# Three blocks on one core: latent keys before first scores, split pieces between heads, turned probabilities copied before rows, square sums after a split

## Chip, cores and metric

The kernel runs on one core of a Trainium2 chip. The metric is the device time of one launch in microseconds (us). TensorE does the matrix products, VectorE (DVE) and ScalarE (ACT) the work on their results, GpSimd (POOL) small steps, SyncE (SP) starts the loads of the weights. The five run their own lists of instructions in order and wait for each other on semaphores.

## What is computed

Three residual blocks over 256 tokens of width 1024, in fp32. The first has MoBA attention and retention, cross attention to a memory, and a gated MLP. The second has a sparse attention with an index, a short convolution and a squared-ReLU MLP. The third has latent attention (MLA) and a squared-ReLU MLP. The part on which most of the change lies is MLA, cut from the reference:

```python
def _mla_mixer(h, rope_mla, w_dq, q_norm, w_uq, w_dkv, kv_norm, w_ukv, w_o):
    q = (_rms_norm(h @ w_dq, q_norm) @ w_uq).reshape(bsz, s, C_HEADS, C_NOPE_DIM + C_ROPE_DIM)
    q_rope = _rotate(q[..., C_NOPE_DIM:], cos, sin)
    kv_a = h @ w_dkv
    c_kv = _rms_norm(kv_a[..., :C_KV_RANK], kv_norm)
    k_rope = _rotate(kv_a[..., C_KV_RANK:][:, :, None, :], cos, sin)[:, :, 0, :]
    kv = (c_kv @ w_ukv).reshape(bsz, s, C_HEADS, C_NOPE_DIM + C_V_DIM)
    k_nope, v = kv[..., :C_NOPE_DIM], kv[..., C_NOPE_DIM:]
    ...
```

There are 16 heads; a head's query and key have 64 elements of their own and 32 rotated ones, and the 32 of the key are the same for all heads. Every sublayer ends in `x = x + rms_norm(...)`.

## The kernel before

**Precision.** A product in fp32 is made of three products in a faster format. Each weight is split into a high part `w_hi` (ScalarE, L630) and a low part `w_lo` (VectorE, L1181, L1184 or L1187 by the kind of weight), and the rows likewise (L648, L1202); TensorE adds hi·hi, lo·hi and hi·lo (`products`, L1786).

**Weights.** They come in units of up to 1 MB through a ring of four: SP loads a unit when VectorE has split the one four places earlier (`w_low`), and ScalarE splits a unit when TensorE has used the one four places earlier (`w_used`). `split_to(u)` in the lists of ScalarE and VectorE marks where unit u is split; its place among the other work is written by hand, and so is all other order. `e` is the first unit of MLA's query weights. Units e to e+5 are the queries' (`uq`), e+6 and e+7 the keys' and values' (`ukv`, four pieces of 512 columns on each engine), e+8 to e+11 the output projection (`odd_out`, two pieces of 1024 columns).

**Attention.** `attention(a, heads)` stands in the lists of three engines and is a pipeline over heads. In step n TensorE makes the scores of head n (L1893), turns the probabilities of head n-2 (L1901) and multiplies those of head n-3 with the values (L1910). VectorE masks the scores and takes their maximum (`masked_max`, L1339; in cross attention L1343 and L1345) and copies the turned probabilities of head n-2 to SBUF (`copy_turned`, L1351); ScalarE makes the exponentials (L801). In the steps H and H+1 behind the last head VectorE also makes the first half of the output rows, of tokens 0 to 127 and then 128 to 255 (`normalise_half`, L1368 and L1369), and TensorE turns them for the output projection (`turn_half`, L1855). `copied()` is TensorE's wait until ScalarE has moved the projection's sums out of PSUM (`evict`, L688).

**MLA's start.** `keys(g)` (L2382) and `values_of(g)` (L2391) make the keys and values of the heads 8g to 8g+7; `copy_keys` and `copy_values` (L1124 and L1129 on ScalarE, L1711 and L1716 on VectorE) bring them to SBUF. `rotate_queries(g, t)` (L1248 to L1253) rotates the queries of half g and tokens t, `turn_heads(g)` (L1855) turns them, and `plain_banks` (L672, L1220) copies these. `spread_rope` on GpSimd (L557) copies the rotated part of the key from head 0 to the other 15 heads.

**Squared MLP.** `first_up` makes the hidden rows of chunk 0 by tokens, ScalarE takes them out (`first_part`, L860), VectorE squares them (L1436); then `second_up` (L2064, L2068) makes chunk 1 from the units u0+2 and u0+3. `boundary` adds the sublayer's output to x, and its two `stream_square` (L710) sum x's squares, for a factor that the MLP needs at its end.

## Time and profile before

| what | value |
|---|---|
| median of 3 runs | 1043.85 us (1043.06 to 1043.96) |
| the profiled execution | 1043.6 us, span of its trace 1041.8 us |
| TensorE busy | 1018.8 us, 98% of the span |
| VectorE, ScalarE, GpSimd busy | 673.0, 568.5 and 87.2 us |
| granted TensorE clock | 0.998 of full speed (2.4 GHz) |
| DMA | 176.32 MB, 169 GB/s on average |

An engine's busy time is the sum of its instructions' spans. The chain that ended last is made of TensorE for 95% of the span, so a microsecond is gained only where TensorE stands idle, or lost where a new wait appears. A row of the view of waits tells for a group of instructions what ended the idle time just before them. In the timeline a row gives start, length, engine, line, operation and the tiles; the bracket at its end is the engine's idle time before it and what ended that.

### The profile page before, as it was taken

The page shows a single profiled execution, that of the slowest core. Times are in us where ns is not written, and L with a number is a line of the kernel's source. Part 1 is how long each engine was busy: PE and PEld are TensorE (multiplying, and loading weights), DVE is VectorE, ACT ScalarE, POOL GpSimd, SP SyncE. Part 2 cuts the span into 40 slices and gives each one's busy share as a digit, 9 for nine tenths or more (in the row PEclk, how much of TensorE's full clock was granted, in tenths as well). Part 3 has the DMA queues.
Part 4 walks back from the last instruction along what each step waited for, and adds up shares of the span by engine and source line. Part 5 has one row for each costly group of instructions (what it writes and reads, how often), then busy time and mean ns, then how long its engine had stood idle before and what let it go on. Part 6 is the DMA issues. An engine that isn't in the chain of part 4 may idle for free.

```text
span 1041.8 us, 14292 instructions
## 1 busy us (share of the span) xinstructions
PE 1018.8 (98%) x5164; PEld 862.5 (83%) x5164; DVE 673.0 (65%) x1083; ACT 568.5 (55%) x909; POOL 87.2 (8%) x117
## 2 busy tenths in 40 slices
PE   7999999999999999999999999999998999999997
PEld 6888888888888888788888888888898888888886
DVE  5575675457556554869856676566579767756663
ACT  7466465427545444766555665455476566554541
POOL 2010001001000000300051200000052001000000
PEclk9999999999999999999999999999999999999999
DMA  9746236315545555463423555554255044654521
GB/s 351 289 162 242 79 114 224 130 41 182 189 175 212 175 205 173 157 239 125 164 117 127 217 202 191 195 182 169 84 189 216 1 162 163 242 196 176 192 81 41
DMA packets 28463, 176.32 MB, mean 169 GB/s; under 512 B 3248, under 2 KB 3392, under 8 KB 9984
## 3 DMA queue, kind: packets, MB, share of 16 engines
q1 hardware_dynamic: 26784, 170.08, 45.1%
q0 software_dynamic: 1456, 5.48, 1.4%
q8 instruction: 30, 0.49, 0.2%
q10 hardware_dynamic: 176, 0.13, 0.0%
q14 instruction: 17, 0.14, 0.0%
HBM read 174.62 MB, written 1.05 MB: 169 GB/s over the span
## 4 chain that ended last, share of the span: by engine, by line
PE 95%; DVE 2%; ACT 1%; issue 1%; DMA 1%; SPq 0%; DVEq 0%; ACTq 0%
PE PS L1786 67%; PE PS L2064 10%; PE PS L2068 5%; PE PS L1855 3%; PE PS L1893 3%; PE PS L1910 3%; PE PS L2298 1%; PE PS L1901 1%; DMA x<-in_x 1%; DVE w_lo L1184 1%; PE PS L2000 0%; ACT w_hi L630 0%; PE PS L2382 0%; PE PS L2391 0%; PE PS L1941 0%
## 5 line engine op out<-in xcount | busy, mean ns | idle before, releaser
L1786 PE MATMUL PS<-w_hi,hT 128*128 128x512 f32 (+2 forms) x1296 | 323.2, 389 | 2.2 <-issue 1.6
L1187 DVE SCALAR_TENSOR_TENSOR w_lo<-w_raw,gcol,w_hi 128x512 fp32r<-128x512 f32 (+4 forms) x318 | 260.9, 879 | 92.3 <-ACT w_hi L630 90.6
L630 ACT ACTIVATE w_hi<-w_raw,gcol 128x512 fp32r<-128x512 f32 (+4 forms) x326 | 244.4, 817 | 96.4 <-PE PS L1786 69.6
L1786 PEld LDWEIGHTS PS<-w_hi,hT 128*128 128x128 f32 x1296 | 237.8, 188 | 47.4 <-issue 1.7
L1181 DVE TENSOR_TENSOR w_lo<-w_raw,w_hi 128x1024 fp32r<-128x1024 f32 x118 | 143.3, 1249 | 91.4 <-ACT w_hi L630 90.4
L630 ACT ACTIVATE w_hi<-w_raw 128x1024 fp32r<-128x1024 f32 x118 | 119.2, 1052 | 102.7 <-PE PS L1786 97.5
L1786 PE MATMUL PS<-w_lo,hT 128*128 128x512 f32 (+2 forms) x648 | 171.8, 384 | 0.0
L2064 PE MATMUL PS<-hT,w_hi 128*128 128x512 f32 x448 | 156.6, 398 | 1.4 <-ACT arena L860 1.4
L1786 PEld LDWEIGHTS PS<-w_lo,hT 128*128 128x128 f32 x648 | 120.8, 188 | 23.6
L2068 PE MATMUL PS<-hT,w_lo 128*128 128x256 f32 x448 | 116.6, 281 | 0.0
L1786 PE MATMUL PS<-w_hi,gT_hi 128*128 128x512 f32 x408 | 114.0, 392 | 0.0
L1786 PE MATMUL PS<-w_lo,gT_hi 128*128 128x512 f32 x408 | 112.7, 389 | 0.0
L1786 PE MATMUL PS<-w_hi,gT_lo 128*128 128x512 f32 x408 | 112.7, 389 | 0.0
L2064 PEld LDWEIGHTS PS<-hT,w_hi 128*128 128x128 f32 x448 | 81.5, 188 | 18.2 <-issue 2.2
L1786 PEld LDWEIGHTS PS<-w_hi,gT_lo 128*128 128x128 f32 x408 | 76.6, 188 | 16.1
L1786 PEld LDWEIGHTS PS<-w_lo,gT_hi 128*128 128x128 f32 x408 | 76.5, 188 | 15.9
L1786 PEld LDWEIGHTS PS<-w_hi,gT_hi 128*128 128x128 f32 x408 | 76.4, 188 | 15.2
L2068 PEld LDWEIGHTS PS<-hT,w_lo 128*128 128x128 f32 x448 | 84.7, 189 | 4.5
L517 POOL TENSOR_SCALAR msq<-ssq 128x1 f32<-128x1 f32 (+1 forms) x31 | 10.5, 338 | 809.6 <-ACT work L710 746.8
L1202 DVE TENSOR_TENSOR hT<-PS,hT 128x512 fp32r<-128x512 f32 (+2 forms) x46 | 29.4, 668 | 29.6 <-ACT hT L648 29.4
L648 ACT ACTIVATE hT<-PS 128x512 fp32r<-128x512 f32 (+2 forms) x46 | 25.4, 582 | 40.7 <-PE PS L1855 40.6
L801 ACT ACTIVATE work<-work,attention_bias 128x128 f32<-128x128 f32 x64 | 28.5, 447 | 27.2 <-DVE attention_bias L1339 27.2
(191 smaller groups left out, 842.8 us busy)
## 6 DMA issues: line engine op xcount, KB each, us to landing
w_raw<-in_w SPq DMA_DIRECT2D x64, 1024.0 KB, 4.8
w_raw<-in_w_gu SPq DMA_DIRECT2D x22, 1024.0 KB, 4.8
w_raw<-in_w_in SPq DMA_DIRECT2D x11, 1024.0 KB, 7.5
w_raw<-in_w_dn SPq DMA_DIRECT2D x22, 512.0 KB, 4.5
w_raw<-in_w_mem_k SPq DMA_DIRECT2D x4, 1024.0 KB, 4.8
w_raw<-in_w_out SPq DMA_DIRECT2D x4, 1024.0 KB, 4.9
w_raw<-in_w_cq SPq DMA_DIRECT2D x4, 1024.0 KB, 4.7
w_raw<-in_w_mem_v SPq DMA_DIRECT2D x4, 1024.0 KB, 4.8
```

What stands on the lines that cost most here:

```text
L630: act.activation(high, source, ACT.Copy, scale=1.0 if col is None else gcol[:, col + TURNED * k:col + TURNED * k + 1])\
L648: act.activation(d, PS[:, 4 + n["tb"] % 4, 0:blocks * P].rearrange("p (b m) -> p b m", m=P), ACT.Copy).then_inc(tb_high, 1)
L801: ins = act.activation(a.E[hd % 3][:, c0:c1], src, ACT.Exp, bias=a.nb[:, hd, t:t + 1], scale=-1.0 if a.masked else a.scale, accum_out=a.su ...
L1181: ins = dve.tensor_tensor(lo, raw, hi, ALU.subtract)
L1187: ins = dve.scalar_tensor_tensor(out=lo, in0=raw, scalar=gcol[:, col + TURNED * k:col + TURNED * k + 1], in1=hi, op0=ALU.mult, op1=ALU.sub ...
L1202: dve.tensor_tensor(lo, PS[:, 4 + n["tb"] % 4, 0:blocks * P].rearrange("p (b m) -> p b m", m=P), hi.bitcast(F32), ALU.subtract).then_inc(t ...
L1786: mm = pe.matmul(bank(t, j)[:, 0:width], rows[:, kc0 + k, tok], w[:, s, at:at + width], start=begin and i == 0, stop=end and i == 2)
L1855: mm = pe.transpose(PS[0:rows, 4 + n["tb"] % 4, i * P:(i + 1) * P], src, ident[:])
L1893: mm = pe.matmul(PS[:, a.score_bank + hd % 2, c0:c1], q, k, start=i == 0, stop=i == len(pairs) - 1)
L1910: mm = pe.matmul(out_banks(a, t)[:, hd * a.dv:(hd + 1) * a.dv], a.ET[hd % 2][:, c0 + s * P:c0 + (s + 1) * P], a.v(hd, s), start=s == 0, st ...
L2064: return pe.matmul(PS[:, 4 + b, :], w_hi[:, s, at:at + P], hT[:, k, :, :].rearrange("p s m -> p (s m)"), start=k == 0, stop=k == KC - 1)
L2068: return pe.matmul(PS[:, 4 + b, 0:SEQ], w_lo[:, s, at:at + P], hT_hi[:, k, :], start=False, stop=False)
```

## The change

It has five parts. (1) In MLA, TensorE makes `values_of(0)` before `turn_heads(1)` and `keys(1)` before the first scores; the waits for copied keys and values are placed later or split by engine, and the rotated key is spread by one DMA that ScalarE starts, in place of five copies on GpSimd. (2) The units e+9, e+10 and e+11 are split in halves, one half ahead of every second head (`split_half`); before, e+9 was split at the start of the heads, and e+10 and e+11 behind them. (3) `copy_turned` stands ahead of `normalise_half`. (4) The wait `copied()` moves in MoBA, cross attention and the sparse attention (`dsa`) to a place inside step 3, ahead of the first values. (5) In the squared MLPs unit u0+3 is split ahead of `first_part(0)`, the sums of x's squares come after that, and `second_up` waits for each of its units only where it uses it.

```diff
@@ gpsimd
-            def spread_rope():
-
-                tb_done(pool, KEY_BANK)
-                for head in range(1, 16, 3):
-                    pool.tensor_copy(kT4[64:96, head:head + 3, :], kT4[64:96, 0:1, :].to_broadcast([32, 3, SEQ])).then_inc(rope_spread, 1)
...
@@ scalar
+            def split_half(u, half):
+
+                assert n["split"] == u and len(pieces(u)) == 2
+                split(u, some=slice(half, half + 1))
+                n["split"] += half
...
-                stream_square(0)
-                stream_square(1)
+                if squares:
+                    stream_square(0)
+                    stream_square(1)
...
+                split_to(m.u0 + 3)
                 first_part(0)
-                split_to(m.u0 + 3)
+                for t in range(TT):
+                    stream_square(t)
                 first_part(1)
...
             high_keys(1)
             split_to(e + 6)
+            act.wait_ge(rope_copied, 1)
+            act.dma_start(kT4[64:96, 1:16, :], kT4[64:96, 0:1, :].to_broadcast([32, 15, SEQ])).then_inc(rope_spread, 16)
             n["used"] += 3
             evict(0, queries(1), query_rows)
...
             copy_keys(0)
             split_to(e + 8)
+            copy_values(0)
             plain_banks(4, heads96(qT4, 1))
-            copy_values(0)
-            split_to(e + 9)
-            attention(mla, [0])
             copy_keys(1)
-            attention(mla, [1])
+            attention(mla, [0, 1])
             copy_values(1)
-            attention(mla, range(2, mla.H), False)
+            attention(mla, [2, 3], False)
+            for k in range(6):
+                split_half(e + 9 + k // 2, k % 2)
+                attention(mla, [4 + 2 * k, 5 + 2 * k], False)
             high_halves(hT_hi)
-            boundary(4)
+            boundary(4, squares=False)
@@ vector
                     if hd < a.H:
                         masked_max(hd)
-                    elif rows is not None:
-                        normalise_half(a, rows, hd - a.H, 0)
                     if hd >= 2:
                         copy_turned(hd - 2)
+                    if hd >= a.H and rows is not None:
+                        normalise_half(a, rows, hd - a.H, 0)
...
+                split_to(m.u0 + 3)
                 first_part(0)
-                split_to(m.u0 + 3)
                 first_part(1)
...
             rotate_queries(1, 0)
+            split_to(e + 7)
             rotate_queries(1, 1)
-            split_to(e + 7)
             n["used"] += 8
             copy_keys(0)
+            copy_values(0)
             plain_banks(4, heads96(qT4, 1))
             split_to(e + 8)
-            copy_values(0)
-            attention(mla, [0])
-            split_to(e + 9)
             copy_keys(1)
-            attention(mla, [1])
+            attention(mla, [0, 1, 2])
             copy_values(1)
-            attention(mla, range(2, mla.H + 2), False, h)
+            attention(mla, [3, 4], False)
+            for k in range(6):
+                split_half(e + 9 + k // 2, k % 2)
+                attention(mla, [5 + 2 * k, 6 + 2 * k], False, h)
+            attention(mla, [mla.H + 1], False, h)
@@ tensor
                         turn_probs(hd - 2)
+                    if hd == 3 and free:
+                        free()
                     if hd >= 3:
                         values(hd - 3)
...
-                    for j in range(2):
-                        high_ready(u + j)
-                        split_ready(u + j)
                     for i, b in enumerate([1, 2, 0, 3]):
                         if i == 1:
                             turn_hidden()
                         pe.wait_ge(m.part if i < 2 else m.low, i % 2 + 1)
                         for j in range(2):
+                            if i == 0:
+                                high_ready(u + j)
+                                split_ready(u + j)
                             mm = up_block(u + j, j, b)
...
-            copied()
-            attention(dsa, [3])
+            attention(dsa, [3], free=copied)
...
             keys(0)
+            copied()
+            values_of(0)
             wait_h(2)
             turn_heads(1)
-            copied()
-            values_of(0)
             pe.wait_ge(keys_copied, 2)
-            pe.wait_ge(rope_spread, 5)
+            keys(1)
+            pe.wait_ge(rope_spread, 16)
             turned(8)
             attention(mla, [0])
-            keys(1)
             attention(mla, [1])
-            pe.wait_ge(values_copied, 2)
+            for t in range(TT):
+                pe.wait_ge(values_copied[t], 1)
             values_of(1)
             attention(mla, [2])
+            pe.wait_ge(values_copied[0], 2)
+            attention(mla, range(3, 8))
             pe.wait_ge(keys_copied, 4)
-            pe.wait_ge(values_copied, 4)
-            attention(mla, range(3, mla.H + 3), h)
+            attention(mla, range(8, 11))
+            pe.wait_ge(values_copied[1], 2)
+            attention(mla, range(11, mla.H + 3), h)
```

MoBA and cross attention get `free=copied` in the same way as `dsa`. VectorE's `split_half` does the low part of the same half as ScalarE's.

The order on TensorE at MLA's start, before (L2382 makes keys, L1855 turns queries, L2391 makes values, L1893 is the first head's scores):

```order
1228 L2382 MATMUL PS<-hT,w_lo 128x256 [waits w_low]
1229 L2382 MATMUL PS<-hT,w_lo 128x256
1230 L1855 MATMUL PS<-ident,h 96x128 [waits tb_free1,h_ready]
...
1237 L1855 MATMUL PS<-ident,h 96x128 x3
1238 L2391 MATMUL PS<-w_hi,hT 128x512 [waits acc_copied]
...
1242 L2391 MATMUL PS<-w_lo,hT 128x512 x2
1243 L1893 MATMUL PS<-arena 128x128 [waits tb_free0,tb_free1,tb_free3,tb_free2,rope_spread,keys_copied]
1244 L1893 MATMUL PS<-arena 128x256
1245 L2382 MATMUL PS<-hT,w_hi 128x256 [waits w_high]
```

The same place in the changed kernel (the lines are now L2401, L2410 and L1873):

```order
1228 L2401 MATMUL PS<-hT,w_lo 128x256 [waits w_low]
1229 L2401 MATMUL PS<-hT,w_lo 128x256
1230 L2410 MATMUL PS<-w_hi,hT 128x512 [waits acc_copied]
...
1234 L2410 MATMUL PS<-w_lo,hT 128x512 x2
1235 L1873 MATMUL PS<-ident,h 96x128 [waits tb_free1,h_ready]
...
1242 L1873 MATMUL PS<-ident,h 96x128 x3
1243 L2401 MATMUL PS<-hT,w_hi 128x256 [waits w_high,keys_copied]
```

The values of the first half stand ahead of the turns of the rotated queries, and the second half's keys behind these and ahead of all scores.

VectorE in MLA's heads 3 to 5, before (L1339 is `masked_max`, L1351 `copy_turned`):

```order
455 L1351 COPY work<-PS 128x384
456 L1339 ISA work,attention_bias<-PS,causal 128x128
457 L1339 ISA attention_bias 128x1
458 L1339 ISA work,attention_bias<-PS,causal 128x256
459 L1339 ISA attention_bias 128x1
460 L1351 COPY work<-PS 128x384
461 L1339 ISA work,attention_bias<-PS,causal 128x128
```

The same in the changed kernel (L1355, L1367), with a piece of the output projection's weights (L1190):

```order
456 L1367 COPY work<-PS 128x384
457 L1190 TENSOR_TENSOR w_lo<-w_raw,w_hi 128x1024
458 L1355 ISA work,attention_bias<-PS,causal 128x128
459 L1355 ISA attention_bias 128x1
460 L1355 ISA work,attention_bias<-PS,causal 128x256
461 L1355 ISA attention_bias 128x1
462 L1367 COPY work<-PS 128x384
```

Such a piece now stands behind every second head's copy, six in all.

VectorE at the end of cross attention, before (L1351 is `copy_turned`, L1368 and L1369 `normalise_half`, L1181 a split):

```order
118 L1351 COPY work<-PS 128x512
119 L1368 RECIPROCAL attention_sum<-attention_sum 128x4
120 L1369 TENSOR_TENSOR h<-PS,attention_sum 128x512
121 L1351 COPY work<-PS 128x512
122 L1369 TENSOR_TENSOR h<-PS,attention_sum 128x512
123 L1351 COPY work<-PS 128x512
124 L1181 TENSOR_TENSOR w_lo<-w_raw,w_hi 128x1024 x2
```

The same in the changed kernel:

```order
118 L1367 COPY work<-PS 128x512 x2
119 L1384 RECIPROCAL attention_sum<-attention_sum 128x4
120 L1385 TENSOR_TENSOR h<-PS,attention_sum 128x512
121 L1367 COPY work<-PS 128x512
122 L1385 TENSOR_TENSOR h<-PS,attention_sum 128x512
123 L1190 TENSOR_TENSOR w_lo<-w_raw,w_hi 128x1024 x2
```

Each of the two last copies stands ahead of the rows it followed.

## Rows read from the trace of the kernel before

**Rows 1.** Waits of TensorE: us in total, times, longest us
```profile
PE PS L1855 <- DVE h L1253: 1.4, 1, 1.4
PE PS L2064 <- ACT arena L860: 1.4, 2, 0.7
PE PS L1893 <- ACT arena L688: 1.2, 1, 1.2
PE PS L1910 <- DVE work L1351: 1.2, 1, 1.2
...
PE PS L1893 <- DVE arena L1220: 0.6, 1, 0.6
PE PS L1893 <- ACT h L688: 0.2, 1, 0.2
```

**Rows 2.** Timeline of cross attention's end: start, length, work, idle before
```profile
206.98 0.60 PE L1901 MATMUL PS<-ident,work 128*128 128x128 f32 x4
...
209.56 0.69 DVE L1369 TENSOR_TENSOR h<-PS,attention_sum 128x512 f32<-128x512 f32 x1
210.16 0.68 DVE L1351 COPY work<-PS 128x512 f32<-128x512 f32 x1
...
214.22 1.28 DVE L1202 TENSOR_TENSOR hT<-PS,hT 128x512 fp32r<-128x512 f32 x2
...
215.15 1.28 PE L1786 MATMUL PS<-w_hi,hT 128*128 128x512 f32 x4
```

**Rows 3.** Timeline of the sparse attention's step 3
```profile
536.33 1.11 ACT L688 ACTIVATE arena<-PS,rstd 128x1024 f32<-128x1024 f32 x1 [0.86 <-PE PS L1786]
...
538.59 0.78 PE L1910 MATMUL PS<-arena,work 128*128 128x64 f32 x6
```

**Rows 4.** Timeline of the first squared MLP's start
```profile
581.42 0.58 ACT L860 ACTIVATE arena<-PS 128x512 f32<-128x512 f32 x1
...
583.12 2.73 DVE L1187 SCALAR_TENSOR_TENSOR w_lo<-w_raw,gcol,w_hi 128x512 fp32r<-128x512 f32 x4
...
586.11 0.47 PE L2064 MATMUL PS<-hT,w_hi 128*128 128x512 f32 x1 [0.68 <-ACT arena L860]
```

**Rows 5.** One line's instructions, all of MLA's key and value splits: ns min/median/max
```profile
L1184 DVE SCALAR_TENSOR_TENSOR w_lo<-w_raw,gcol,w_hi x8: 744/747/1312, 782.3 to 792.8; 128x512 fp32r<-128x512 f32 x8
```

**Rows 6.** Timeline of MLA's start and of its output projection's
```profile
782.57 5.72 POOL L557 COPY arena<-arena 32x768 f32<-32x768 f32 x5 [5.47 <-DVE hT L1202]
...
792.66 1.17 PE L2391 MATMUL PS<-w_hi,hT 128*128 128x512 f32 x4
...
804.53 0.60 ACT L1129 ACTIVATE arena<-PS 128x512 f32<-128x512 f32 x1
...
805.23 0.89 PE L1893 MATMUL PS<-arena 128*128 128x128 f32 x4 [0.76 <-issue]
...
831.33 1.17 PE L1786 MATMUL PS<-w_hi,hT 128*128 128x512 f32 x4 [0.41 <-issue]
```

**Rows 7.** Timeline of one head of MLA
```profile
808.38 0.55 DVE L1351 COPY work<-PS 128x384 f32<-128x384 f32 x1
...
809.47 0.29 DVE L1339 CUSTOM_DVE_ANT_0 work<-PS,causal 128x128 f32<-128x128 f32 x1 [0.54 <-PE PS L1893]
809.60 0.78 PE L1910 MATMUL PS<-arena,work 128*128 128x64 f32 x6
...
809.87 0.40 ACT L801 ACTIVATE work<-work,attention_bias 128x128 f32<-128x128 f32 x1 [0.67 <-DVE attention_bias L1339]
...
811.25 0.78 PE L1910 MATMUL PS<-arena,work 128*128 128x64 f32 x6
```

**Rows 8.** Page, costliest groups: count, busy us, mean ns, idle before
```profile
L1181 DVE TENSOR_TENSOR w_lo<-w_raw,w_hi 128x1024 fp32r<-128x1024 f32 x118 | 143.3, 1249 | 91.4 <-ACT w_hi L630 90.4
L630 ACT ACTIVATE w_hi<-w_raw 128x1024 fp32r<-128x1024 f32 x118 | 119.2, 1052 | 102.7 <-PE PS L1786 97.5
```

**Rows 9.** Page, DMA issues: count, KB each, us from issue to landing
```profile
arena<-in_decay POOLq DMA_DIRECT2D x1, 512.0 KB, 10.8
```

More of the change, by code:

```diff
@@ L1167, in _, with split @@
             n = {"split": 0, "tb": 0, "high": 0, "copied": 0, "used": 0}
-            def split(u, it=None):
+            def split(u, it=None, some=range(KC)):
                 if u >= COUNT:
@@ L1174, in split @@
                 done = 0
-                for cols in pieces(u):
+                for part, cols in enumerate(pieces(u)):
+                    if part not in some:
+                        done += 1
+                        continue
                     lo, raw, hi = w_lo[:, u % RING, cols], w_raw[:, u % RAW, cols], w_hi[:, u % RING, cols].bitcast(F32)
@@ L1194, in split_to, with split_half @@
                     n["split"] += 1
+            def split_half(u, half):
+                assert n["split"] == u and len(pieces(u)) == 2
+                split(u, some=[half])
+                n["split"] += half
             def low_banks(count, dst):
@@ L2224, in _ @@
             attention(moba, [2])
-            copied()
-            attention(moba, range(3, moba.H + 3))
+            attention(moba, range(3, moba.H + 3), free=copied)
             retention(lambda: turn_half(mix, 0))
@@ L2252, in _ @@
             attention(cross, [2])
-            copied()
-            attention(cross, range(3, cross.H + 3), h)
+            attention(cross, range(3, cross.H + 3), h, copied)
             out_project(h)
```

27 lines of the change are left out of this document (13 added, 14 removed).

## Prediction

> **What bounds the kernel now.** I read the chain that ended last first: it is TensorE for nearly all of the span, so an edit on another engine counts only by a wait of TensorE that it removes or makes. The second view is therefore TensorE's own waits [rows 1]. Behind the start-up of the kernel they are short and few: 1.4 us for a rotation on VectorE (L1253, MLA), 1.4 us in two pieces for ScalarE's L860 (one in each squared MLP), 1.2 us for ScalarE's L688 (sparse attention), 1.2 us for VectorE's copy L1351 (cross attention), 0.6 us for the copy of turned queries L1220 (MLA), 0.2 us for L688 (MoBA). Two more are put down to "issue" and stand in the timeline of MLA: 0.76 us before the scores of head 3 and 0.41 us before the output projection [rows 6]. Together 7.2 us, 0.7% of the time. That is the ceiling, since the change leaves TensorE's products as they are and removes none. The third view is the timeline at each of these places, for what really ended the wait and what is late next.
>
> **Cross attention: copies ahead of rows.** The probabilities of head 2 are turned at 206.98, 0.60 us long, but VectorE waits for values before it makes rows at 209.56, and copies head 2 only at 210.16 [rows 2]. TensorE waits 1.2 us for that copy [rows 1]. With the copy ahead of the rows it runs at about 207.6 and the whole wait goes; TensorE would stand 1.3 us earlier behind head 3 (210.90, where its values began, less 209.6, where its turns end), and reach the output projection at 215.15 - 1.3 = 213.8. Late next is VectorE: its queue from the rows on is shorter by one copy, 0.6 us, so L1202, which makes the low part of the first rows, moves from 214.22 to 213.6, and its first half (0.64 us) ends at 214.3. The projection starts at 214.4 and not at 213.8: **0.75 us** of gain, not 1.3. Bounds: 0.6 (VectorE's shift alone) and 1.3.
>
> **Sparse attention: the wait `copied()` inside step 3.** The eviction L688 runs from 536.33 for 1.11 us, TensorE waits for it with the scores of head 3 and multiplies the first values at 538.59 [rows 3]. Only those values write what is being evicted. With the wait ahead of them the scores and turns, 1.1 us up to 538.59, fill the wait; their inputs, exponentials of heads 1 and 2 and VectorE's maxima, are older than the eviction. The values start at 537.5: **1.1 us**, bounds 0.8 and 1.2. What stands behind on ScalarE (the exponentials of head 3) has the gate's eight transposes as cover. In MoBA the same edit meets 0.2 us [rows 1], but there the exponentials of head 1 stand behind the eviction on ScalarE, and TensorE's next step needs them; I take nothing, at most 0.2 us. In cross attention the eviction is over when it is waited for: nothing.
>
> **Squared MLPs: split ahead, sums behind.** TensorE's wait of 0.68 us before `second_up` is put down to the second L860. It asks only for the first, whose row is at 581.42; what ended last for it is the split of u0+3 on VectorE, 583.12 and 2.73 us long, up to 585.85 [rows 4]. That split was late because ScalarE summed x's squares before it made the high part. Now the high part comes 2.5 us earlier, VectorE's low part follows the one before it without a break and ends at about 585.3, and TensorE asks for it only half a block (1.4 us) after its start. Both cover the 0.68 us. The sums are now between two steps on ScalarE, where about 3 us were split and idle time; VectorE's first square slips by nearly 3 us to 586.0, but is needed at 588.3, after TensorE's first block. Twice 0.68: **1.35 us**, bounds 0.7 and 1.4. Nothing on TensorE asks for the sums before the MLP's end.
>
> **MLA's start.** The waits of 1.4, 0.6 and 0.76 us go if nothing new is late: 2.8 us. The first one: values, twelve products of which four take 1.17 us [rows 6], some 3.0 us in all, now stand ahead of the turns that need the rotation. The rotation in its turn comes later, since a unit of four pieces stands before its second half: 4 x 0.68 = 2.7 us. It also comes earlier: the pieces of a unit took 744 to 1312 ns [rows 5], and the slow four lay beside GpSimd's copies from 782.57 on, 5.72 us long [rows 6]; without those copies I take 1.7 us off. The wait would be 1.4 + 2.7 - 1.7 - 3.0, below zero by 0.6. The Trainium skill ("SBUF — State Buffer", "Who interferes with whom") says that a VectorE instruction with two SBUF inputs contends with a GpSimd instruction that reads SBUF; by that rule, the trace agrees, and by its reverse (the pieces stay slow) the wait would be 1.1 us and the MLA term smaller by as much. The second wait, 0.6 us, now has the whole group of the second keys before it and goes. The third: scores of head 3 began when ScalarE's copy of values, 804.53 and 0.60 long, was done [rows 6]. It still waits for that copy, but this one now stands behind the exponentials of head 1, which start some 2.5 us earlier; I get 802.5 for its end and 802.4 for the scores. So the start gives **2.7 us**.
>
> **MLA's heads: pieces between.** A head takes 1.65 us (809.60 to 811.25), in which VectorE idles 0.54 and ScalarE 0.67 us [rows 7]. For two heads VectorE has 1.08 us free and gets a piece of 1249 ns, ScalarE 1.34 and gets 1052 [rows 8]; queued operations overlap by about 0.1 us, so both just fit. But the two are linked in a ring: VectorE's piece (1.14) delays the next maximum, the exponential starts 0.40 later (809.47 to 809.87), two heads' halves take 0.9, then ScalarE's next piece (1.08) before VectorE's next: 3.5 us, against 3.3 us for two heads. The slack of a copy, from 808.93 to its use at 809.60, absorbs the first piece or two; then about 0.15 us is lost for each of four pieces: 0.6 us. At the end the delay of 0.8 us meets the values of head 13, which no longer have a group of scores ahead of them as cover: 0.9 us. Copies ahead of rows return 0.4 us there, and the first half of the second bank's rows comes 0.2 us late in the projection. Sum of MLA: 2.7 - 0.6 - 0.9 + 0.4 - 0.2 = **1.4 us**. Bounds: 2.8 (pieces cost nothing) and -0.5 (a piece costs each of six pairs 0.2 us more than taken and the rotation is late by 0.8). Units e+10 and e+11 leave the place behind the heads, where TensorE did not wait for them: nothing. The DMA that replaces GpSimd's copies costs ScalarE its issue and the wait for one VectorE copy, some 0.5 us ahead of an eviction that nobody needs for 2 us.
>
> **Sum.** 0.75 + 1.1 + 1.35 + 1.4 = 4.6 us. The profiled execution took 1043.6 us, so 1039.0; the median of before is 0.25 us above that execution: **1039.3 us**.
>
> **Rivals.** (a) The pieces are free: the ring has more slack than I give it. For it: each engine alone has room. Against it: the ring's sum of 3.5 us. Then MLA gives 2.8 and the time is 1037.9. (b) The pieces fill VectorE: beside ScalarE's pieces and TensorE's traffic they take 1.3 us and more, as the slow ones in rows 5 did beside another engine, and the rotation is late too. MLA gives about -0.5, the time is 1041.2. (c) The gains are given back: an earlier TensorE meets other waits, for instance for splits or loads behind the boundaries. For it: several places where splits end shortly before their use. Against it: from the boundaries to the loops no wait of more than 0.7 us is shown, and loads have slack. About 1042.7. (d) Slower: the DMA of the rotated key is late. TensorE cannot begin any score without it. It is issued at about 782.1 (GpSimd's copies, which wait for the same row, began at 782.57 [rows 6]), when SP's queue loads weights, and moves 480 KB in rows of 1 KB; the first scores are reached at about 797 (802.4 less the second values and three heads' scores), 15 us later. The slowest comparable row, 512 KB in 10.8 us [rows 9], fits. From 797 every us late is a us lost, after 19.7 us the whole gain of 4.6 is gone, at 24 us of landing the time is 1048. The Trainium skill ("DMA: Bandwidth & Descriptors", "Rules for kernel authors") states that two transfers issued from two engines share the same DMA engines with their packets interleaved; by it the DMA takes turns with the 1 MB loads, which bears on (d), and no run here shows it yet. (e) The edits don't reach the chip as described: the order of instructions shows all of them, so I give it nothing.
>
> **Chances.** Forecast 0.60, (a) 0.13, (b) 0.14, (c) 0.08, (d) 0.05. The forecast's own bounds are 1038.3 to 1040.6. The range takes in most of (a) and (b): 1037.5 to 1041.6. A difference under 0.2% (2.1 us) can't be told from no change here. Faster than 1041.8 are the forecast, (a) and most of (b): 0.83; within are (c) and the rest of (b): 0.12; slower is (d): 0.05.
>
> **What would show it.** In TensorE's waits, the rows for L1253, L1220, L860 and L688 of the sparse attention are gone. In cross attention the projection starts 0.75 us earlier against the head's copy, after a wait for L1202 of about 0.5 us. In MLA, head 3's scores start 2.7 us sooner after the first keys than before, then pairs of heads take 3.3 to 3.5 us with waits of 0.15 us for L1351 in every second head, and one of near 0.9 us at head 13's values. The pieces of L1184 are all near 745 ns. Wrong would be: slow pieces with no GpSimd beside them, pairs at 3.7 us or more, or a wait for the DMA before the first scores.

## The result, and the profile after

The changed kernel took 1037.28 us (median of 4 runs, 1036.58 to 1038.33) beside 1043.87 us for the kernel before on the same chip: ratio 0.9937, 95% interval 0.9925 to 0.9949. A second set, beside the experiments, gave 1038.43 us (5 runs, 1037.40 to 1039.03) beside 1044.05: ratio 0.9943, 0.9929 to 0.9956. So the change gains 5.6 to 6.6 us. The forecast was 4.6 us and 1039.3 us, its range began at 1037.5: the direction was right, the size too small. The profiled execution took 1036.75 us, its trace spans 1034.9 us, with a granted clock of 0.999.

**Waits.** What ended TensorE's idle time in the changed kernel, behind its first load (columns: engine, tile and line, releaser, us in total, times, longest). Lines of the changed kernel: L1804 is the products' old L1786, L1913 the scores, L1921 the turns, L1930 the values, L1367 the copy of turned probabilities, L1385 the rows, L1873 the turns of rows.

```profile
PE PS L1804 <- issue: 1.5, 3, 0.6
PE PS L1804 <- DVE arena L1711: 0.7, 1, 0.7
PE PS L1930 <- DVE work L1367: 0.6, 1, 0.6
PE PS L1873 <- DMA x<-in_x: 0.5, 1, 0.5
PE PS L1930 <- ACT arena L688: 0.2, 1, 0.2
PE PS L1873 <- DVE h L1385: 0.2, 1, 0.2
```

Against [rows 1], the waits for the rotation (L1253), for L1220, the two for L860 and the one for L688 in MoBA are gone; of the one for L688 in the sparse attention 0.2 us is left and has moved to the values. The 0.6 us for L1367 is another wait than in rows 1: it stands at the values of MLA's head 13 and no longer in cross attention. Of the first row, 0.34 us is new and stands in cross attention; the other 1.15 us of it, in two waits, and the 0.7 us for L1711 stand in the kernel before as well. The change does not reach them, and the 7.2 us of the prediction leave them out.

**Where the time went.** TensorE's work is the same in both kernels but for its order at three places, so equal groups of products can be laid side by side: start before less start after. That difference grows where the change gains. It steps by 0.26 us at MoBA's step 3, by 0.80 in cross attention, 1.0 in the sparse attention and 0.93 in the first squared MLP. In MLA it rises by 3.4 us up to the scores of head 3, falls by 0.9 over the heads and by 0.7 at head 13's values, and rises by 0.4 in the output projection; the second squared MLP adds 0.9. Before all of these there is a step of 0.8 us within the first 16 us of the kernel, where the change edits nothing.

**The start-up.** TensorE's timeline there, the kernel before first (start us, length us, engine, line, operation, tiles, count), then two executions of the changed kernel, the one of the prediction's result and a second one:

```profile
11.38 2.06 PE L1786 MATMUL PS<-w_hi,hT 128*128 128x512 f32 x4
...
14.77 0.62 PE L1786 MATMUL PS<-w_lo,hT 128*128 128x512 f32 x2
```

```profile
11.22 1.53 PE L1804 MATMUL PS<-w_hi,hT 128*128 128x512 f32 x4
...
13.95 0.62 PE L1804 MATMUL PS<-w_lo,hT 128*128 128x512 f32 x2
```

```profile
11.34 2.06 PE L1804 MATMUL PS<-w_hi,hT 128*128 128x512 f32 x4
...
15.57 0.62 PE L1804 MATMUL PS<-w_lo,hT 128*128 128x512 f32 x2
```

The last row of each is the same pair of products. In the first execution of the changed kernel it begins at 13.95 us, in the second at 15.57, and behind it the two are shifted by 1.62 us and nothing else up to the end. The spans are 1034.9 and 1036.6 us. So the part of a span from this pair to the end is the measure that tells kernels apart: 1027.0 us before (1041.8 - 14.77), 1021.0 after (1034.9 - 13.95, and 1036.6 - 15.57). The change is worth **6.0 us**, and 0.8 us of the difference between the two first traces is chance of the start-up. I call this part "the rest".

### The profile page after: what moved, and what is told of

It reads as the page before. It is cut to its first block, busy times and chain, and to the rows that moved or that the text cites. A ratio compares the mean times of both kernels' runs of the same rounds, so it can differ in the third digit from the quotient of the medians.

```text
span 1034.9 us, 14294 instructions
## 1 busy us (share of the span) xinstructions
PE 1018.0 (98%) x5164; PEld 862.4 (83%) x5164; DVE 670.3 (65%) x1083; ACT 568.0 (55%) x909; POOL 82.4 (8%) x112
## 4 chain that ended last, share of the span: by engine, by line
PE 94%; ACT 2%; DVE 1%; issue 1%; DMA 1%; SPq 0%; DVEq 0%; ACTq 0%
PE PS L1804 68%; PE PS L2086 10%; PE PS L2090 5%; PE PS L1873 4%; PE PS L1913 2%; PE PS L1930 2%; PE PS L2318 1%; ACT w_hi L624 1%; PE PS L1921 1%; DMA x<-in_x 1%; ACT work L802 1%; PE PS L2401 1%; PE PS L2410 1%; PE PS L2022 0%; PE PS L1963 0%
## 5 line engine op out<-in xcount | busy, mean ns | idle before, releaser
L1804 PE MATMUL PS<-w_hi,hT 128*128 128x512 f32 (+2 forms) x1296 | 322.6, 389 | 2.2 <-issue 1.5
L1804 PEld LDWEIGHTS PS<-w_hi,hT 128*128 128x128 f32 x1296 | 237.5, 188 | 47.6 <-issue 1.5
L1190 DVE TENSOR_TENSOR w_lo<-w_raw,w_hi 128x1024 fp32r<-128x1024 f32 x118 | 143.7, 1250 | 92.4 <-ACT w_hi L624 91.5
L1804 PE MATMUL PS<-w_lo,hT 128*128 128x512 f32 (+2 forms) x648 | 171.6, 384 | 0.0
L1804 PEld LDWEIGHTS PS<-w_lo,hT 128*128 128x128 f32 x648 | 120.5, 188 | 23.5
L1804 PE MATMUL PS<-w_hi,gT_hi 128*128 128x512 f32 x408 | 114.0, 392 | 0.0
L1804 PE MATMUL PS<-w_lo,gT_hi 128*128 128x512 f32 x408 | 112.8, 389 | 0.0
L1804 PE MATMUL PS<-w_hi,gT_lo 128*128 128x512 f32 x408 | 112.7, 389 | 0.0
L1804 PEld LDWEIGHTS PS<-w_hi,gT_lo 128*128 128x128 f32 x408 | 76.6, 188 | 16.1
L1804 PEld LDWEIGHTS PS<-w_lo,gT_hi 128*128 128x128 f32 x408 | 76.5, 188 | 15.9
L1804 PEld LDWEIGHTS PS<-w_hi,gT_hi 128*128 128x128 f32 x408 | 76.4, 188 | 15.3
L518 POOL TENSOR_SCALAR msq<-ssq 128x1 f32<-128x1 f32 (+1 forms) x31 | 12.6, 405 | 815.0 <-ACT work L710 752.4
```

Of the source, the lines that this page charges most:

```text
L1190: ins = dve.tensor_tensor(lo, raw, hi, ALU.subtract)
L1804: mm = pe.matmul(bank(t, j)[:, 0:width], rows[:, kc0 + k, tok], w[:, s, at:at + width], start=begin and i == 0, stop=end and i == 2)
```

## Experiments

The edits are to the changed kernel. "Gives" is the rest of the trace, less 1021.0.

| run | median us | ratio to before, 95% interval | pair at us | rest us | gives us |
|---|---|---|---|---|---|
| before (profile) | 1043.87 | 1 | 14.77 | 1027.0 | +6.0 |
| the changed kernel | 1037.28 | 0.9937 (0.9925 to 0.9949) | 13.95 | 1021.0 | 0 |
| after_again | 1038.43 | 0.9943 (0.9929 to 0.9956) | 15.57 | 1021.0 | 0.0 |
| u_mlp | 1039.63 | 0.9961 (0.9947 to 0.9975) | 14.10 | 1022.9 | +1.9 |
| u_free | 1039.20 | 0.9956 (0.9940 to 0.9973) | 14.77 | 1022.3 | +1.3 |
| u_copy | 1039.14 | 0.9949 (0.9933 to 0.9966) | 15.47 | 1022.1 | +1.1 |
| u_mla | 1040.61 | 0.9966 (0.9954 to 0.9979) | 15.26 | 1023.4 | +2.4 |
| pool_spread | 1039.33 | 0.9955 (0.9939 to 0.9970) | 14.84 | 1022.8 | +1.8 |
| ring_cut | 1037.13 | 0.9933 (0.9918 to 0.9948) | 15.37 | 1020.0 | -1.0 |
| behind | 1040.09 | 0.9960 (0.9946 to 0.9975) | 14.83 | 1024.2 | +3.2 |
| two | 1037.16 | 0.9934 (0.9918 to 0.9949) | 14.70 | 1020.2 | -0.8 |
| two_cut | 1037.58 | 0.9932 (0.9918 to 0.9946) | 16.13 | 1020.0 | -1.0 |
| warm | 1037.80 | 0.9944 (0.9930 to 0.9957) | 14.90 | 1021.0 | 0.0 |
| best | 1036.44 | 0.9930 (0.9916 to 0.9944) | 14.89 | 1019.7 | -1.3 |

The theory of the prediction is that each wait is worth what its row shows. The rival, formed from the two traces, is that a row shows some 0.2 us less than the wait costs.

**One part undone: the squared MLPs (u_mlp).** ScalarE's list; VectorE's split and TensorE's waits for the two units went back in the same way, and the sums of x's squares to the boundary.

```diff
-                split_to(m.u0 + 3)
                 first_part(0)
-                for t in range(TT):
-                    stream_square(t)
+                split_to(m.u0 + 3)
                 first_part(1)
```

> The changed kernel with its part in the two squared MLPs undone: split of the fourth unit between the two halves of the first step again, square sums back ahead of the split, both unit waits ahead of the first block. Two theories. A, the prediction's sizes: each MLP gives back the 0.68 us that the timeline shows as idle ahead of the second up products, so the span grows by 1.35 us and the time comes to about 1038.6. B, an idle row shows less than the wait costs, because TensorE's rows are drawn to their modelled end and the next product would start before it: each MLP loses 0.9 us, together 1.8 us, about 1039.1. In the trace, against the changed kernel, the second up products come 0.7 us later by A and 0.9 by B, in both MLPs, and an idle row of about 0.7 is shown by both.

Measured: 0.93 us in the first MLP and 0.94 in the second, 1.9 together: B. How the row falls short can be read from TensorE's timeline at `second_up`, with the part undone (bracket: idle time before and what ended it) and then in the changed kernel:

```profile
581.67 1.07 PE L1803 MATMUL PS<-w_lo,hT 128*128 128x512 f32 x4
583.43 0.47 PE L2085 MATMUL PS<-hT,w_hi 128*128 128x512 f32 x1 [0.69 <-ACT arena L862]
583.73 0.40 PE L2089 MATMUL PS<-hT,w_lo 128*128 128x256 f32 x2
```

```profile
581.48 1.07 PE L1804 MATMUL PS<-w_lo,hT 128*128 128x512 f32 x4
582.39 0.39 PE L2086 MATMUL PS<-hT,w_hi 128*128 128x512 f32 x1
582.61 0.40 PE L2090 MATMUL PS<-hT,w_lo 128*128 128x256 f32 x2
```

From the start of the four products to the next one it is 1.76 us with the wait and 0.91 us without it, although their row is 1.07 us long in both: the next product starts 0.16 us before the row's end, so the bracket, 0.69, shows 0.16 too little. Behind the wait the first product has 0.30 us to the next, without it 0.22: 0.08 more. 0.69 + 0.16 + 0.08 = 0.93. The Trainium skill ("Perfetto Trace Analysis", "Summary: the profiler window per engine type") says that the end of a TensorE instruction in a profile is an estimate; by that, the trace agrees, with the 0.16 us here.

**One part undone: the wait inside step 3 (u_free).** MoBA and cross attention were changed back in the same way.

```diff
-            attention(dsa, [3], free=copied)
+            copied()
+            attention(dsa, [3])
```

> The changed kernel with one part undone: in MoBA, cross and sparse attention the wait for the eviction of the last projection stands ahead of step 3 of the heads again and no longer inside it. A, the prediction's sizes: sparse attention loses 1.1 us, MoBA and cross nothing, time about 1037.9. B, waits are larger than shown, and MoBA's shown 0.2 us is a real wait: sparse attention loses 1.0 to 1.1, MoBA 0.26, cross nothing, about 1038.1. What tells A from B is the shift of TensorE's work behind MoBA's step 3 against the changed kernel: 0.0 by A, 0.26 by B.

Measured: 0.26 us in MoBA, nothing in cross attention, 1.0 us in the sparse attention. The rows with the part undone:

```profile
106.78 0.92 PE L1913 MATMUL PS<-arena 128*128 128x128 f32 x4 [0.22 <-ACT h L688]
...
536.78 0.92 PE L1913 MATMUL PS<-arena 128*128 128x128 f32 x4 [1.21 <-ACT arena L688]
```

and in the changed kernel MoBA's values, with no bracket, and those of the sparse attention, with what is left of it, and under them ScalarE's last exponential before MoBA's eviction, the eviction and the next exponential:

```profile
106.66 0.85 PE L1930 MATMUL PS<-arena,work 128*128 128x64 f32 x6
...
535.61 0.88 PE L1930 MATMUL PS<-arena,work 128*128 128x64 f32 x6 [0.22 <-ACT arena L688]
```

```profile
103.91 0.49 ACT L802 ACTIVATE work<-work,attention_bias 128x256 f32<-128x256 f32 x1
...
104.75 1.11 ACT L688 ACTIVATE h<-PS,rstd 128x1024 f32<-128x1024 f32 x1 [0.25 <-PE PS L1804]
105.76 0.39 ACT L802 ACTIVATE work<-work,attention_bias 128x128 f32<-128x128 f32 x1
```

TensorE's next turns (106.19 us) are those of head 1, and the exponentials at 103.5 to 104.4 us are head 1's: they stand ahead of the eviction. Only head 2's stand behind it. B holds in MoBA. With the part undone MoBA's bracket of 0.22 us costs 0.26 and not 0.46 us, because the changed kernel still has a wait there that no bracket shows: its values start 0.47 us behind the turns and take 0.69 to the next scores, where later heads have 0.33 and 0.62. They start at 106.66, just behind VectorE's copy for them, which ends at 106.51.

**One part undone: copies ahead of rows (u_copy).**

```diff
-                    if hd >= 2:
-                        copy_turned(hd - 2)
                     if hd >= a.H and rows is not None:
                         normalise_half(a, rows, hd - a.H, 0)
+                    if hd >= 2:
+                        copy_turned(hd - 2)
```

> The changed kernel with one part undone: at the two steps behind the last head of cross attention and MLA, VectorE makes rows before it copies the turned probabilities again. A, the prediction's sizes: cross loses 0.75 us and MLA 0.4, time 1037.9. B, shown waits are 0.15 to 0.25 short: cross loses 0.8 to 1.0, MLA 0.4 to 0.6, 1038.0 to 1038.3. C, the pieces have changed the end of MLA so far (VectorE is late there anyway) that the order of copy and rows no longer matters there: MLA 0.0, cross 0.8, 1037.6.

Measured: 0.83 us in cross attention, where A said 0.75 and B 0.8 to 1.0, and 0.2 us in MLA, less than A's 0.4 and more than C's nothing. In the changed kernel VectorE's copy of head 2 now stands at 206.53 us, ahead of the first rows, and that of head 3 at 209.08, ahead of the second; TensorE waits before the projection instead:

```profile
206.53 0.69 DVE L1367 COPY work<-PS 128x512 f32<-128x512 f32 x1 [1.11 <-PE PS L1921]
...
208.47 0.69 DVE L1385 TENSOR_TENSOR h<-PS,attention_sum 128x512 f32<-128x512 f32 x1
209.08 0.68 DVE L1367 COPY work<-PS 128x512 f32<-128x512 f32 x1
209.67 0.68 DVE L1385 TENSOR_TENSOR h<-PS,attention_sum 128x512 f32<-128x512 f32 x1
...
213.33 1.17 PE L1804 MATMUL PS<-w_hi,hT 128*128 128x512 f32 x4 [0.34 <-issue]
```

**One part undone: all of MLA's own (u_mla).** The order of splits and copies, `values_of` behind `turn_heads`, no pieces between heads, and the rotated key spread by GpSimd; ScalarE's list is shown, the others went back with it:

```diff
-            copy_values(0)
             plain_banks(4, heads96(qT4, 1))
+            copy_values(0)
+            split_to(e + 9)
+            attention(mla, [0])
             copy_keys(1)
-            attention(mla, [0, 1])
+            attention(mla, [1])
             copy_values(1)
-            attention(mla, [2, 3], False)
-            for k in range(6):
-                split_half(e + 9 + k // 2, k % 2)
-                attention(mla, [4 + 2 * k, 5 + 2 * k], False)
+            attention(mla, range(2, mla.H), False)
```

> The changed kernel with all of MLA's own part undone (order of splits and copies in its start, values before turned queries, pieces between heads, rope keys spread by GpSimd again and not by a DMA); the order of copies and rows, the MLPs, and the other attentions stay changed. A, the prediction's sizes: MLA gives back 1.0 us of the 1.4 (the 0.4 of copies ahead of rows stays), time about 1037.8. B, what the two traces show: start 3.3 us back, pieces' loss of 1.6 back, together 1.7 to 2.1 us, about 1038.6. In the trace VectorE's pieces beside GpSimd's copies take 1.3 us again, TensorE stands 3.3 us later at the first scores of MLA than in the changed kernel, and pairs of heads take 3.3 us instead of 3.5.

Measured: 2.4 us, a little more than B. The start is worth 3.5 us, the pairs of heads give back 0.9 and head 13's values 0.7, and then the undone kernel loses 0.4 to 0.5 us again, in two waits for VectorE's rows:

```profile
827.62 0.66 PE L1875 MATMUL PS<-ident,h 128*128 128x128 f32 x4 [0.39 <-DVE h L1389]
...
830.58 1.20 PE L1806 MATMUL PS<-w_hi,hT 128*128 128x512 f32 x4 [0.24 <-DVE h L1389]
```

This kernel has copies ahead of rows, the kernel before has rows ahead of copies, and its TensorE leads that kernel's by 2.2 us through MLA's heads and by 2.1 us in the output projection: without pieces the order of copies and rows is worth nothing in MLA.

What each wait of the start cost can be read by the same distances between starts as in `second_up`: from the kernel before, against the same kinds of products without a wait in the changed kernel. The bracket of 1.42 us ahead of the turns cost 1.64 us, the one of 0.64 ahead of the first scores 0.87, and the one of 0.76 ahead of head 3's scores 1.00: 3.5 us in all, 0.22 to 0.24 more than each bracket. Of this the changed kernel loses 0.17 us again at the values of head 0, in a wait without a bracket.

**GpSimd's copies in place of the DMA (pool_spread).**

```diff
+                for head in range(1, 16, 3):
+                    pool.tensor_copy(kT4[64:96, head:head + 3, :], kT4[64:96, 0:1, :].to_broadcast([32, 3, SEQ])).then_inc(rope_spread, 1)
...
-            act.dma_start(kT4[64:96, 1:16, :], kT4[64:96, 0:1, :].to_broadcast([32, 15, SEQ])).then_inc(rope_spread, 16)
```

> The changed kernel with the rotated key spread to its fifteen heads by five GpSimd copies, as before, in place of the DMA; the rest stays changed. A, GpSimd slows VectorE beside it (before: pieces of 1.31 us instead of 0.75): VectorE's pieces of the unit between the two halves of the rotation take 1.2 to 1.3 us, the rotation ends about 2 us later than 787.8, and TensorE waits for it, 0.8 to 1.3 us, before the second turns; the DMA is what makes the start worth 3.4 us instead of about 2.3. B, the slow pieces have another cause (their own place beside weight loads): they stay at 0.75 us without or with GpSimd, and the time is that of the changed kernel within 0.2 us.

Measured: 1.7 us lost by the shifts (1.8 by the rest), 0.3 ahead of the first values' products and 1.3 at the second turns: A, and a little more. The slow pieces are those of the unit ahead of the rotation's halves, not the one between them (POOL's five copies, VectorE's four pieces beside them and the next four, and TensorE's wait):

```profile
779.35 5.75 POOL L558 COPY arena<-arena 32x768 f32<-32x768 f32 x5 [5.00 <-DVE arena L1758]
779.57 4.83 DVE L1198 SCALAR_TENSOR_TENSOR w_lo<-w_raw,gcol,w_hi 128x512 fp32r<-128x512 f32 x4
...
786.85 2.74 DVE L1198 SCALAR_TENSOR_TENSOR w_lo<-w_raw,gcol,w_hi 128x512 fp32r<-128x512 f32 x4
...
790.98 1.19 PE L1878 MATMUL PS<-ident,h 128*96 128x128 f32 x9 [1.11 <-DVE h L1274]
```

With the DMA all eight pieces take the short time, and it lands before anyone needs it (the issues of the stretch, with KB and us from issue to landing, and VectorE's pieces by form):

```profile
arena<-arena ACTq DMA_DIRECT2D x1, 480.0 KB, 10.9
```

```profile
L1193 DVE SCALAR_TENSOR_TENSOR w_lo<-w_raw,gcol,w_hi 128x512 fp32r<-128x512 f32 x8 | 5.5, 746 | 0.0
```

**ScalarE's pieces one head earlier (ring_cut).**

```diff
-            attention(mla, [2, 3], False)
             for k in range(6):
+                attention(mla, [2] if k == 0 else [1 + 2 * k, 2 + 2 * k], False)
                 split_half(e + 9 + k // 2, k % 2)
-                attention(mla, [4 + 2 * k, 5 + 2 * k], False)
+            attention(mla, range(13, mla.H), False)
```

> The changed kernel with ScalarE's piece of each unit one head earlier among MLA's heads (behind the exponentials of head 2, 4, 6 ...), VectorE's left where they are, so that VectorE's low part no longer waits for a high part made just before it. A, the ring of the two engines costs the time (VectorE's pieces stood idle 0.23 us for ScalarE's): pairs of heads return from 3.49 to 3.31 us, TensorE gains 0.9 us over five pairs and most of the 0.6 us wait at the values of head 13; about 1.0 to 1.4 us less than the changed kernel. B, the engines are simply full (a piece of about 1.25 us does not fit between the steps of two heads on VectorE wherever ScalarE's lies): pairs stay at 3.45 to 3.5 and the gain is below 0.3 us.

Measured: pairs at 3.31 us, 1.0 us gained, 0.4 us left of the wait at head 13: A. In the changed kernel a pair takes 3.50 us (here 804.16 to 807.66 between two groups of values), with no idle row on TensorE. The 0.19 us that it loses lie in waits too short for a bracket: the values of every second head start 0.41 us behind the turns and take 0.72 us to the next scores (from 807.25), those of the head between 0.33 and 0.62 (from 805.59).

```profile
804.16 0.88 PE L1930 MATMUL PS<-arena,work 128*128 128x64 f32 x6
...
805.59 0.49 PE L1921 MATMUL PS<-ident,work 128*128 128x128 f32 x3
805.92 0.78 PE L1930 MATMUL PS<-arena,work 128*128 128x64 f32 x6
806.54 0.87 PE L1913 MATMUL PS<-arena 128*128 128x128 f32 x4
807.25 0.49 PE L1921 MATMUL PS<-ident,work 128*128 128x128 f32 x3
807.66 0.88 PE L1930 MATMUL PS<-arena,work 128*128 128x64 f32 x6
808.38 0.87 PE L1913 MATMUL PS<-arena 128*128 128x128 f32 x4
...
821.63 0.88 PE L1930 MATMUL PS<-arena,work 128*128 128x64 f32 x6 [0.62 <-DVE work L1367]
```

Each piece of VectorE waits for ScalarE's:

```profile
805.36 1.23 DVE L1190 TENSOR_TENSOR w_lo<-w_raw,w_hi 128x1024 fp32r<-128x1024 f32 x1 [0.23 <-ACT w_hi L624]
...
808.85 1.23 DVE L1190 TENSOR_TENSOR w_lo<-w_raw,w_hi 128x1024 fp32r<-128x1024 f32 x1 [0.23 <-ACT w_hi L624]
```

With ScalarE ahead they start without a wait, 3.31 us apart:

```profile
806.48 1.22 DVE L1190 TENSOR_TENSOR w_lo<-w_raw,w_hi 128x1024 fp32r<-128x1024 f32 x1
806.74 1.04 ACT L624 ACTIVATE w_hi<-w_raw 128x1024 fp32r<-128x1024 f32 x1
...
809.79 1.22 DVE L1190 TENSOR_TENSOR w_lo<-w_raw,w_hi 128x1024 fp32r<-128x1024 f32 x1
```

**No pieces between the heads (behind).** The loops with `split_half` became plain `attention` calls on both engines.

> The changed kernel without pieces between MLA's heads: the split of the first output unit, too, now stands behind the heads, on both engines. A, only the pieces slow the heads: pairs take 3.31 us, no wait at head 13's values, TensorE reaches the output projection 1.5 us earlier than in the changed kernel (about 823.9), but then stands about 3 us for the second unit's low part, since VectorE makes rows first; in all 1 to 2 us slower than the changed kernel. B, the slow pairs come from the copies' place or the earlier start and not from the pieces: pairs stay at 3.49 and the wait at head 13 stays.

Measured: A for the heads, whose pairs take 3.31 us with no wait at head 13's values, but not for what follows. TensorE gains 1.5 us up to the projection and then loses 4.7 us, and 3.2 us are lost in all where A said 1 to 2. It stands 2.6 us for ScalarE's high part of an output unit, where A said 3 us for VectorE's low part, and loses more behind that:

```profile
PE PS L1799 <- ACT w_hi L624: 2.6, 1, 2.6
```

**Two pieces only (two_cut, two).** In two_cut, on ScalarE:

```diff
-            attention(mla, [2, 3], False)
-            for k in range(6):
-                split_half(e + 9 + k // 2, k % 2)
-                attention(mla, [4 + 2 * k, 5 + 2 * k], False)
+            for k in range(2):
+                attention(mla, [2] if k == 0 else [1 + 2 * k, 2 + 2 * k], False)
+                split_half(e + 9, k)
+            attention(mla, range(5, mla.H), False)
```

> A version meant to beat both: only the two pieces of the first output unit stand between MLA's heads (VectorE before heads 5 and 7 of its count, ScalarE one head earlier, behind heads 2 and 4), the other four pieces stand behind the heads again, where the kernel before had them and TensorE did not wait for them. A, each piece between heads costs: the last pairs run at 3.31 us, nothing is left to wait at head 13's values (ScalarE ahead alone left 0.4), gain against the changed kernel 1.3 to 1.6 us, of which 0 to 0.2 is returned by rows in the projection; time about 1037.0 where the changed kernel repeated gives 1038.4. B, the other two units are late behind the heads, since the heads end 1.5 us sooner than in the kernel before: TensorE waits 1 us or more for the third or fourth unit in the projection and the gain is gone, about 1038.4.

> As the run two_cut, but ScalarE's two pieces stay where the changed kernel has them, ahead of VectorE's by no head. A, two pieces are absorbed by the slack of the heads that follow: pairs with a piece take 3.49 us (two times 0.19 lost), the others 3.31, no wait at head 13; 0.1 to 0.4 us slower than two_cut. B, the delay once made is never given back but costs nothing more either: same time as two_cut within 0.1 us.

Measured: two_cut reaches the projection 1.5 us earlier than the changed kernel, as by A, but 0.44 us is given back by rows and later units (expected 0 to 0.2), so it gains 1.0, no more than ring_cut. In `two`, the pairs with a piece lose 0.33 us in all; it gives back the same and gains 0.8. A, with the give-back as the miss.

**TensorE kept busy before the first load (warm).**

```diff
+            dve.memset(hT[:, 7, :, :].bitcast(F32), 0.0).then_inc(warm_ready, 1)
...
+            for _ in range(9):
+                pe.matmul(PS[:, 7, :], hT[:, 7, 1, 0:P], hT[:, 7, :, :], start=True, stop=True)
```

> The changed kernel with one addition at its very start: VectorE fills an unused part of the hidden rows' tile with zeros, and TensorE multiplies it nine times (128x512) into a bank that is overwritten later, while it otherwise waits 5.6 to 6.3 us for the first loads. It tests where the start-up's chance shift of 0 to 2.2 us comes from. A, TensorE's speed: in the traces the products of the first unit take 0.46 us each up to a point between 12.4 and 16 us and 0.23 us after it; with TensorE busy from 1 us on they take 0.23 us from the first on, the first output of the second weight piece stands at 12.9 us or earlier in place of 13.95 to 16.13, the gain is 1 to 2 us against the changed kernel repeated, and the times of single runs spread less. B, the late start is one of loads and of the engines that split them: products wait for w_in's pieces instead, the groups stand where they stood (13.95 to 16.1), gain below 0.3 us.

Measured: neither mechanism. The nine products started 0.43 us apart behind the first, and those of the first unit still did so up to 13.4 us, with a granted clock of 1.00 in the rows of every stretch. No idle time stands between the rows of the first unit, so they did not wait for weights, as B has it. The pair stands at 14.90, among the earlier values, and nothing is gained: B's number without B's cause. The expectation's "0.23 us from the first on" failed.

```profile
1.47 4.21 PE L2231 MATMUL PS<-hT 128*128 128x512 f32 x9 [1.47 <-DVE hT L1175]
...
11.53 2.06 PE L1806 MATMUL PS<-w_hi,hT 128*128 128x512 f32 x4
13.38 0.76 PE L1806 MATMUL PS<-w_lo,hT 128*128 128x512 f32 x2
13.97 1.09 PE L1806 MATMUL PS<-w_hi,hT 128*128 128x512 f32 x4
```

**The version that beats both (best).** It has the addition of `warm`, and among MLA's heads:

```diff
+            for k in range(4):
+                attention(mla, [2] if k == 0 else [1 + 2 * k, 2 + 2 * k], False)
+                split_half(e + 9 + k // 2, k % 2)
+            attention(mla, range(9, mla.H), False)
```

> A version meant to beat both: the changed kernel with the addition of the run warm, and among MLA's heads four pieces instead of six, ScalarE's one head earlier than in the changed kernel, the last unit's two pieces behind the heads. A, the gains add: against the run warm 1.0 to 1.3 us (no wait at head 13's values, pairs at 3.31 us but for the start-up of the ring, 0.1 to 0.3 given back by rows and the last unit in the projection). B, VectorE's rows behind the last head bound the projection whatever the heads do: gain against the run warm 0.7 us or less.

Measured: A. Its rest is 1.3 us shorter than that of `warm` and of the changed kernel; the medians are 1036.44 and 1037.80 us. The intervals of the two ratios overlap, so it is the traces that tell them apart. No wait is left at head 13; what bounds now are VectorE's rows:

```profile
823.74 0.65 PE L1875 MATMUL PS<-ident,h 128*128 128x128 f32 x4 [0.39 <-DVE h L1387]
...
826.69 1.20 PE L1806 MATMUL PS<-w_hi,hT 128*128 128x512 f32 x4 [0.24 <-DVE h L1387]
```

## The prediction, step by step

| term | forecast us | measured us | by |
|---|---|---|---|
| MoBA, wait inside step 3 | 0 | 0.26 | u_free |
| cross, copies ahead of rows | 0.75 | 0.8 | u_copy |
| sparse attention, wait inside step 3 | 1.1 | 1.0 | u_free |
| squared MLPs | 1.35 | 1.8 to 1.9 | traces, u_mlp |
| MLA, start | 2.7 | 3.3 to 3.5 | traces, u_mla |
| MLA, pieces in pairs of heads | -0.6 | -0.9 | traces, ring_cut |
| MLA, head 13's values | -0.9 | -0.7 | traces, behind |
| MLA, behind the heads | +0.2 | +0.4 | traces |
| sum | 4.6 | 6.0 to 6.3 | rest: 6.0 |

**What held.** The order of things: each wait of rows 1 that was said to go went, the rotation stopped being waited for, GpSimd's copies were what slowed VectorE's pieces (pool_spread: 4.83 us for four pieces beside them, 2.74 for four without), the DMA took 10.9 us where rows 9 gave 10.8, the pieces made a ring that costs the heads, and its end met head 13. In cross attention both the gain and the wait that takes its place (0.34 us, "about 0.5" was said) came as worked out. Rival (d) did not come: the DMA's landing is nearly 4 us ahead of the first scores. Rival (a), free pieces, is excluded by ring_cut and behind, and (b), slow pieces, by the 1.23 us of their rows; (c) by the shifts, which stay constant behind the boundaries.

**Step that failed: "what its row shows" as the price of a wait.** The ceiling of "7.2 us" and the terms "twice 0.68" and "2.8 us" for MLA's start took brackets at face value. A wait is worth its bracket plus 0.16 us by which the row of the products before it is drawn too long, plus 0.08 for the first product behind it. For the MLPs that is 2 x 0.93 in place of 1.35, measured 1.8 to 1.9. For MLA's start the three waits cost 3.5 us in place of 2.8, less 0.17 us that is lost again at head 0's values: 3.3 to 3.5 measured. Two terms, some 1.2 us: most of the miss of 1.4. In the sparse attention it is hidden, since the 1.21 us bracket of u_free with its 0.24 would be 1.45, and the changed kernel still has a bracket of 0.22, 0.46 by the same sum: 1.0, as measured.

**Step that failed: MoBA's exponentials.** I had head 1's exponentials behind the eviction and took nothing; they stand ahead of it, and 0.26 us was gained.

**Mis-sized, and cancelling.** The pairs lose 0.15 us with the first piece and 0.19 in each of the four pairs behind it, not 0.15 after one or two free ones: the slack of a copy absorbs nothing, and the waits of 0.15 us that were to be seen in every second head are too short for a bracket. Head 13 costs 0.7 and not 0.9, and of that some 0.4 is cover for VectorE's rows: take it away (u_mla, behind, two_cut, best) and TensorE waits 0.39 and 0.24 us for rows, where the changed kernel waits 0.19. The 0.4 us that copies ahead of rows were to return in MLA are not there: undoing that order cost 0.2 us with the pieces and nothing without them. The net cost of the pieces is therefore 0.9 + 0.7 - 0.4 = 1.2 us, and `best` regains 1.3.

**Chance.** With the measured 6.0 us the forecast would have been 1037.8. The median of the first set was 0.5 us below that, the one of the second 0.6 above: where a run falls depends on its start-up, which I had not given any width, and the 0.2 us by which the first set lies below the range's low end of 1037.5 are within it. Rival (a) named 1037.9 us and 6.0 us of gain, which is what was measured, by luck: its pieces were to be free and cost 1.2 us net, and the waits were worth about that much more than it said.

## What to carry to other kernels

Price a wait of TensorE by the distance between the starts of the products around it, with and without the wait, not by the idle time that a row shows; several short waits then add up to more than the sum of their rows, and a wait too short for a row still costs. If two engines pass pieces to each other between steps that also link them, let the one that makes the input run a step ahead: the work stays, the ring goes. Before naming a gain of a microsecond, lay two executions of the same kernel side by side and see where they differ.

## What the runs showed of the hardware

- An idle row behind TensorE's products falls short by 0.16 us of 128x512 products' overlap, and the first product behind a wait takes 0.30 us to the next where 0.22 is usual. In the two waits of the squared MLPs and the three of MLA's start, with products of other forms among them, the cost was 0.22 to 0.24 us above the row. A wait of 0.08 us has no row and cost 0.19 us, with the 0.10 us that the values behind it took longer.
- At the start of the kernel 128x512 products start 0.43 us apart, about the pace of the 1.2 GHz level, and later 0.23 us apart, that of the 2.4 GHz level, while the rows give a granted clock of 1.00 in both stretches. Where it changes differs between executions: the pair of products above began anywhere from 13.95 to 16.13 us in 14 traces, the two earliest (13.95 and 14.10) being those with the shortest idle time before the second tile of x (0.54 and 0.38 us; 0.7 to 1.0 in the others). Nine products before the first load, 4.2 us of them, did not bring the change forward. What sets it is open. The Trainium skill ("TensorE: Matmul & The Clock Gate", "What's actually happening") says that the number of slow products at a kernel's start differs from run to run; the two executions of the changed kernel agree, with two and nine products that took more than 0.3 us to the next.
- GpSimd's copies of 32x768 beside VectorE's operation with two SBUF inputs made the four pieces 1.2 us each in place of 0.75. The Trainium skill ("SBUF — State Buffer", "Who interferes with whom") has this as a rule; by it, the trace agrees.
- A copy within SBUF of 480 KB into 32 partitions took 10.9 us beside weight loads, as long as a 512 KB load did [rows 9].
